# Low halves of every second weight unit on GpSimd instead of VectorE, in the third stage of a streaming encoder layer

## The chip, the cores and the metric

One core of a Trainium2 chip runs the whole program. The metric is device time in microseconds (us) of one execution, the median of several.

## The reference, cut to what matters

One layer over 544 tokens (512 prompt frames and 32 frames of a running stream), width 2048: a combined projection, a convolution branch, an attention branch, a merge, and then a product-key expert layer. The change touches the end of the expert layer:

```python
idx = jnp.take_along_axis(cidx, j, axis=-1)      # 8 heads x 16 experts of 16384 for each token
g = jax.nn.softmax(sc, axis=-1)
ue, ve = u_tab[idx], v_tab[idx]
a = jnp.einsum('td,thkd->thk', xb, ue).astype(f32)
wgt = (g * jax.nn.gelu(a, approximate=False)).astype(xb.dtype)
return jnp.einsum('thk,thkd->td', wgt, ve)
```

All arithmetic is held to float32 accuracy, so the kernel splits each operand of a product in a high half, which TensorE takes exactly, and a low half, the rest, and adds three products.

## The kernel before, in words

All weights stream from HBM in units of 128 x 2048 floats (1 MB): z, attention out, convolution out, merge out and query units first, then 128 units of `peer_u`, then 128 of `peer_v`. Two slots hold raw units (`w_raw`), two the high halves (`w_hi`), two the low halves (`w_lo`). Of a unit: SyncE loads it (line 360, in `load_w`) when the low half of the unit two before it is there, ScalarE rounds it to the high half (line 645) when TensorE is done with the unit two before, and VectorE or GpSimd subtracts (the low half), then TensorE uses it.

Who makes the low half: GpSimd up to the first 42 units of `peer_u`, in four pieces of 512 columns (`lo`, line 590), VectorE in one piece from there on (`split`, line 1319).

The experts are applied in two ways. For 384 tokens all 16384 experts are computed densely by TensorE. For the other 160 the 128 chosen rows of each token are fetched by GpSimd with indirect DMAs (`fetch`, line 618, 1 MB each, 160 slots for the `peer_u` rows and 160 for the `peer_v` rows, three row buffers), and VectorE multiplies them in: `dot` for `peer_u`, `gather_add` (line 1400) for `peer_v`.

The third stage, dense product with `peer_v`, runs over 16 groups of 8 units (0 to 7). In a unit TensorE makes two tiles of 24 matmuls each (line 1822, PSUM `ST`), each of which VectorE adds to `acc` (lines 1384, 1386), and TensorE doesn't begin a tile before the one of the same bank in the unit before has been added. VectorE's order in a unit n of `group` is written out by hand: addition of the first tile; in units 3 to 6 two preparations of the next group's activations (`prep`, lines 1360, 1363, 1365: gate times activation, high half, low half); addition of the second tile; the gathers that `V_SLOTS` puts there; the split of unit n + 2; in group 14 also two residual additions (line 1392). The number of gathers in a group is 8 in group 0, 12 in 1 to 3, 11 in 4, 6, 8, 10, 12 and 14, 10 in 5, 7, 9, 11 and 13, and 0 in 15: one a unit, and a second one in units 0, 2, 1 and 7, in this order, as far as the number asks for it.

GpSimd has only the fetches in this stage: fetch j waits for the gather of j - 3 (`row_taken`), whose buffer it fills. SyncE loads weights, and after each group's eighth weight load, once the eight preparations are done (`w_prepped`), it issues the next gates and activations, `load_ag` (lines 519 and 521, 1.5 MB each), in the same queue as the weights. In group 14 it also has line 559. After group 14 VectorE copies the gathered sums to `rows` (line 1459) and TensorE turns them (line 1838) before group 15. In group 3 VectorE hands over the sums of 32 tokens (`b_handed`), which TensorE turns before group 4 (line 1830).

Of the kernel before, what the change touches and what calls it, by code (L numbers as in the profile page):

```python
# [49 lines left out]
U_PU = U_PQ + NQ  # L50
U_PV = U_PU + NU
# [4 lines left out]
GRP = 8  # L56
NGRP = NKEY // GRP
# [9 lines left out]
SLOTS = SA + SB  # L67
TAIL_DOTS = (2, 2, 2, 2, 2, 1, 1, 1, 1, 1, 1)
V_SLOTS = (8, 12, 12, 12) + (11, 10) * 5 + (11, 0)
NG = 3  # L70
DOTS = 12
LOOP_SLOTS = 21
U_G0 = 42
# [36 lines left out]
def build(nc, w_all, x_t, consts, late, params, lams, keys_t, past_k, past_v, hist,  # L110
          y_t, k_t, v_n, cst_p, cst_s):
    ctx = ExitStack()
    with ctx:
# [168 lines left out]
        def sem(name):  # L282
            return ctx.enter_context(nc.semaphore(name))
# [3 lines left out]
        hi_ready, lo_ready = sem("hi_ready"), sem("lo_ready")  # L287
# [52 lines left out]
        def slot(j):  # L340

            return j if j < SLOTS else (j - SLOTS + SA) % SLOTS

        def slots_at(g, n):

            c, first = V_SLOTS[g], sum(V_SLOTS[:g])
            per = [1 if c else 0] * GRP
            for x in (0, 2, 1, 7)[:max(c - GRP, 0)]:
                per[x] += 1
            first += sum(per[:n])  # L350
            return list(range(first, first + per[n]))
# [224 lines left out]
        @block.gpsimd  # L576
        def _(pool):
            pool.memset(u[:, 0:HIST], 0.0).then_inc(u_zeroed, 1)

            def lo_whole(w, slot):  # L580
                pool.wait_ge(hi_ready, w + 1)
                pool.tensor_tensor(w_lo[:, slot, :], raw[:, slot, :], w_hi[:, slot, :].bitcast(F32), ALU.subtract)\
                    .then_inc(lo_ready, 1)

            def lo(w, slot, nth):

                pool.wait_ge(hi_ready, w + 1)
                for q in range(4):
                    cols = slice(q * UNITW // 4, (q + 1) * UNITW // 4)
                    ins = pool.tensor_tensor(w_lo[:, slot, cols], raw[:, slot, cols], w_hi[:, slot, cols].bitcast(F32), ALU.subtract)  # L590
                    if q < 3:
                        ins.then_inc(lo_part, 1)
                    else:
                        pool.wait_ge(lo_part, nth)
                        ins.then_inc(lo_ready, 1)

            for k in range(1, KD, 2):
                pool.wait_ge(x_loaded[k // 4], 16)
                pool.tensor_tensor(xsq[:, k, :], xs[:, k, :], xs[:, k, :], ALU.mult).then_inc(xsq_pool, 1)
                if k == KD // 2 - 1:  # L600
                    lo_whole(0, 0)
            lo_whole(1, 1)
            with pool.Fori(1, U_PU // 2 + 1) as v:
                for n in range(2):
                    lo(v * 2 + n, n, v * 6 + (3 * n - 3))

            with pool.Fori(0, U_G0 // 2 - 1) as v:
                for n in range(2):
                    lo(v * 2 + (n + U_PU + 2), n, v * 6 + 3 * (n + U_PU + 1))
            nth = 3 * (U_PU + U_G0 - 1)  # L610
            lo(U_PU + U_G0, 0, nth)

            def fetch(j):

                if j >= NG:
                    pool.wait_ge(row_taken, j - NG + 1)
                table = u_rows.rearrange("c b i q n -> (c b i) (q n)") if j < SLOTS else v_rows.rearrange("g c p d -> (g c p) d")
                pool.indirect_dma_start(rows[j % NG][:, :], None, table,  # L618
                                        bass.IndirectOffsetOnAxis(v_idx[:, slot(j):slot(j) + 1], 0))\
                    .then_inc(row_loaded[j % NG], 16)  # L620

            pool.wait_ge(idx_ready, 1 + BG)
            for s in u_stored:
                pool.wait_ge(s, 64 * NKEY // 2 + 1)
            pool.wait_ge(scores_taken, TT)
            pool.wait_ge(chosen, TT)
            for j in range(SLOTS):
                fetch(j)
            pool.wait_ge(rows_stored, 16 * NV)
            for j in range(SLOTS, 2 * SLOTS):  # L630
                fetch(j)


        @block.scalar
# [255 lines left out]
        def _(dve):  # L890
# [154 lines left out]
            with dve.Fori(0, NH // 2) as hp:  # L1045
                own.loop(hp, 2 * per_head)
                turns = iter(range(32))
                for r in range(2):
                    h = hp * 2 + r
                    g = h * STEPS  # L1050
# [265 lines left out]
            def split(un, slot):  # L1316
                dve.wait_ge(hi_ready, un + 1)
                dve.wait_ge(lo_ready, un)
                V.tensor_tensor(w_lo[:, slot, :], raw[:, slot, :], w_hi[:, slot, :].bitcast(F32), ALU.subtract)\  # L1319
                    .then_inc(lo_ready, 1)  # L1320
# [37 lines left out]
            def prep(parity, c):  # L1358
                a = a_st[:, c, :]
                own.by(V.tensor_tensor(a.rearrange("p (b n) -> p b n", n=GB), a.rearrange("p (b n) -> p b n", n=GB),  # L1360
                                       gl_st[:, :, c, :], ALU.mult))
                settle()
                own.by(V.tensor_copy(wt_hi[parity][:, c, :], a))  # L1363
                settle()
                V.tensor_tensor(wt_lo[parity][:, c, :], a, wt_hi[parity][:, c, :].bitcast(F32), ALU.subtract).then_inc(w_prepped, 1)
# [15 lines left out]
            def add(q, d, k, first):  # L1381
                dve.wait_ge(tile_done, q + (2 * KD + 1))
                if first:
                    V.tensor_copy(acc[:, d, 0:NT], PD[k]).then_inc(acc_added, 1)
                else:
                    V.tensor_tensor(acc[:, d, 0:NT], PD[k], acc[:, d, 0:NT], ALU.add).then_inc(acc_added, 1)  # L1386

            def residual(d):

                dve.wait_ge(xr_loaded[d % 2], 16 * (d // 2 + 1))  # L1390
                dve.wait_ge(acc_added, (NGRP - 2) * KD + (d + 3))
                V.tensor_tensor(acc[:, d, 0:NT], gb[:, d % 2, :], acc[:, d, 0:NT], ALU.add).then_inc(xr_taken, 1)

            def gather_add(x, v):

                j = SLOTS + x
                dve.wait_ge(row_loaded[j % NG], v * (16 * LOOP_SLOTS // NG) + 16 * (j // NG + 1))
                dve.wait_ge(row_taken, v * LOOP_SLOTS + j)
                col = slot(j) if x < SB else v * LOOP_SLOTS + slot(j)
                V.scalar_tensor_tensor(acc_g, rows[j % NG][:, :], w_g[:, bass.ds(col, 1)], acc_g, ALU.mult, ALU.add)\  # L1400
                    .then_inc(row_taken, 1)
# [18 lines left out]
            def group(g, g0, v, more, splits, pre=None, first=False, last=False):  # L1420

                parity = g0 % 2
                for n in range(GRP):
                    for k in range(2):
                        q = g * KD + (2 * n + k)
                        dve.wait_ge(acc_added, q + 1)
                        add(q, 2 * n + k, k, first)
                        if k == 0 and more and 3 <= n < 7:
                            if n == 3:
                                dve.wait_ge(al_loaded, g * 16 + 16)  # L1430
                                dve.wait_ge(gl_loaded, g * 16 + 16)
                            prep(1 - parity, 2 * (n - 3))
                            prep(1 - parity, 2 * (n - 3) + 1)
                    if pre and n in pre:
                        pre[n]()
                    for s in slots_at(g0, n):
                        gather_add(s, v)
                    if n < splits:
                        split(g * GRP + (n + U_PV + 2), n % 2)
                    if last:  # L1440
                        residual(2 * n)
                        residual(2 * n + 1)
# [6 lines left out]
            for g in range(4):  # L1449
                group(g, g, 0, True, GRP, {0: b_handed} if g == 3 else None, first=(g == 0))  # L1450
            with dve.Fori(0, (NGRP - 6) // 2) as v:
                own.loop(v, 4 * GRP)
                for b in range(2):
                    group(v * 2 + (b + 4), b + 4, v, True, GRP)
# [6 lines left out]
            def take_back():  # L1461
# [5 lines left out]
                    .then_inc(acc_g_added, 1)  # L1467

            group(NGRP - 2, NGRP - 2, 0, True, GRP, None, last=True)
            hand_over()  # L1470
            dve.wait_ge(xr_taken, KD)
# [462 lines left out]
```

## Time and profile before

| what | us |
| --- | --- |
| median of 3 runs | 4139.95 (4130.86 to 4145.09) |
| the profiled execution, its own time | 4146.39 |
| its span, first to last instruction | 4144.5 |
| TensorE matmuls busy | 3902.2 (94%) |
| VectorE busy | 3103.3 (75%) |
| GpSimd busy | 1372.6 (33%) |
| ScalarE busy | 1057.3 (26%) |
| VectorE's splits, line 1319, 213 of them | 487.3 |
| GpSimd's pieces, line 590, 612 of them | 841.1 |
| third stage, line 1822 | from 2950.6 to 4141 |

The profile is of one execution; the table's busy times are of its span. A busy share is an average over stages with different limits. TensorE's matmuls overlap each other, so that a matmul's own duration (about 0.33 us in this stage) is nearly twice the distance from one to the next. GpSimd's busy time counts its pieces and the writing of its DMA descriptors. Idle time of an engine that nothing waits for costs nothing.

### The profile page before, as it was taken

The page shows a single profiled execution, that of the slowest core. Times are in us where ns is not written, and L with a number is a line of the kernel's source. Part 1 is how long each engine was busy: PE and PEld are TensorE (multiplying, and loading weights), DVE is VectorE, ACT ScalarE, POOL GpSimd, SP SyncE. Part 2 cuts the span into 40 slices and gives each one's busy share as a digit, 9 for nine tenths or more (in the row PEclk, how much of TensorE's full clock was granted, in tenths as well). Part 3 has the DMA queues.
Part 4 walks back from the last instruction along what each step waited for, and adds up shares of the span by engine and source line. Part 5 has one row for each costly group of instructions (what it writes and reads, how often), then busy time and mean ns, then how long its engine had stood idle before and what let it go on. Part 6 is the DMA issues. An engine that isn't in the chain of part 4 may idle for free.

```text
span 4144.5 us, 68649 instructions
## 1 busy us (share of the span) xinstructions
PE 3902.2 (94%) x25123; PEld 3823.2 (92%) x25123; DVE 3103.3 (75%) x4273; ACT 1057.3 (26%) x1096; POOL 1372.6 (33%) x947
## 2 busy tenths in 40 slices
PE   7999999999999998999999999999998989999988
PEld 7889888898899998989999999999998989999988
DVE  6877877788776413477869999996788878888785
ACT  3222222232223112222233333332212222222211
POOL 3333333333334443465642222222133323323220
PEclk9999999999999998999999999999999999999999
DMA  7998989979978986876769999999688887887884
GB/s 284 315 341 307 325 291 351 335 274 345 344 247 290 345 311 227 281 263 229 249 242 387 386 377 392 381 389 385 244 333 309 310 314 292 325 312 296 322 302 150
DMA packets 451447, 1285.21 MB, mean 310 GB/s; under 512 B 34128, under 2 KB 258128, under 8 KB 343120
## 3 DMA queue, kind: packets, MB, share of 16 engines
q1 hardware_dynamic: 372336, 876.99, 59.6%
q0 software_dynamic: 46080, 335.56, 20.9%
q10 hardware_dynamic: 32832, 70.07, 4.4%
q8 instruction: 117, 1.92, 0.2%
q14 instruction: 82, 0.67, 0.0%
HBM read 1070.18 MB, written 345.75 MB: 342 GB/s over the span
## 4 chain that ended last, share of the span: by engine, by line
PE 45%; DVE 17%; issue 16%; DMA 11%; POOL 5%; SPq 3%; ACT 1%; DVEq 1%; POOLq 0%; ACTq 0%
PE ST L1732 17%; PE PA L1489 16%; PE ST L1822 9%; DMA w_raw<-w_all 6%; POOL w_lo L590 5%; DVE w_lo L1319 4%; DMA u_rows<-u_out 4%; DVE xg L1023 3%; DVE PA L1400 2%; PE ST L1797 2%; SPq L389 1%; DVE a_st L1360 1%; DVE u_out L926 1%; DVE acc L1386 1%; DVE wt_hi L1363 1%
## 5 line engine op out<-in xcount | busy, mean ns | idle before, releaser
L590 POOL TENSOR_TENSOR w_lo<-w_raw,w_hi 128x512 fp32r<-128x512 f32 x612 | 841.1, 1406 | 1243.4 <-ACT w_hi L645 1243.4
L645 ACT ACTIVATE w_hi<-w_raw 128x2048 fp32r<-128x2048 f32 x368 | 703.4, 1912 | 1451.7 <-PE ST L1822 634.5
L1822 PE MATMUL ST<-wt_hi,w_hi 128*128 128x384 f32 x2048 | 698.9, 341 | 77.2 <-DVE acc L1386 74.4
L1822 PE MATMUL ST<-wt_lo,w_hi 128*128 128x384 f32 x2048 | 695.4, 340 | 0.0
L1822 PE MATMUL ST<-wt_hi,w_lo 128*128 128x384 f32 x2048 | 694.6, 339 | 0.0
L1319 DVE TENSOR_TENSOR w_lo<-w_raw,w_hi 128x2048 fp32r<-128x2048 f32 x213 | 487.3, 2288 | 189.0 <-ACT w_hi L645 189.0
L618 POOL DMA_INDIRECT rows<-v_rows,v_idx x160 | 331.8, 2074 | 813.4 <-DVE PA L1400 783.2
L1489 PE MATMUL PA<-h_hi,w_hi 128*128 128x272 f32 x2496 | 546.3, 301 | 6.4 <-POOL w_lo L590 6.4
L1489 PE MATMUL PA<-h_hi,w_lo 128*128 128x272 f32 x2496 | 527.0, 293 | 0.0
L1489 PE MATMUL PA<-h_lo,w_hi 128*128 128x272 f32 x2496 | 526.4, 293 | 0.0
L1732 PE MATMUL ST<-h_hi,w_hi 128*128 128x384 f32 x1408 | 509.6, 362 | 5.9 <-DVE w_lo L1319 4.3
L1732 PE MATMUL ST<-h_hi,w_lo 128*128 128x384 f32 x1408 | 476.4, 338 | 0.0
L1732 PE MATMUL ST<-h_lo,w_hi 128*128 128x384 f32 x1408 | 474.6, 337 | 0.0
L1822 PEld LDWEIGHTS ST<-wt_hi,w_hi 128*128 128x128 f32 x2048 | 393.2, 192 | 85.1 <-DVE acc L1386 42.0
L1489 PEld LDWEIGHTS PA<-h_hi,w_hi 128*128 128x128 f32 x2496 | 405.5, 194 | 13.2 <-issue 6.7
L926 DVE STREAM_TRANSPOSE u_out<-u_in 128x2048 f32<-128x2048 f32 x128 | 294.9, 2306 | 162.0 <-DMA u_rows<-u_out 153.0
L1489 PEld LDWEIGHTS PA<-h_lo,w_hi 128*128 128x128 f32 x2496 | 404.1, 194 | 0.0
L1489 PEld LDWEIGHTS PA<-h_hi,w_lo 128*128 128x128 f32 x2496 | 401.2, 194 | 0.0
L1822 PEld LDWEIGHTS ST<-wt_lo,w_hi 128*128 128x128 f32 x2048 | 393.0, 192 | 0.0
L1822 PEld LDWEIGHTS ST<-wt_hi,w_lo 128*128 128x128 f32 x2048 | 392.9, 192 | 0.0
L1400 DVE SCALAR_TENSOR_TENSOR PA<-rows,w_g,PA 128x2048 f32<-128x2048 f32 x160 | 375.8, 2349 | 5.3 <-DVE PA L1400 0.8
L618 POOL DMA_INDIRECT rows<-u_rows,v_idx x160 | 178.2, 1114 | 600.7 <-DVE rows L1327 593.6
(271 smaller groups left out, 6293.2 us busy)
## 6 DMA issues: line engine op xcount, KB each, us to landing
w_raw<-w_all SPq DMA_DIRECT2D x368, 1024.0 KB
u_in<-w_all SPq DMA_DIRECT2D x128, 1024.0 KB, 8.5
u_rows<-u_out SPq DMA_DIRECT2D x512, 256.0 KB, 7.4
v_rows<-w_all SPq DMA_DIRECT2D x128, 1024.0 KB, 9.1
a_scr<-gb ACTq DMA_DIRECT2D x128, 192.0 KB
g_scr<-g_st ACTq DMA_DIRECT2D x24, 1024.0 KB, 12.0
a_st<-a_scr SPq DMA_DIRECT2D x15, 1536.0 KB, 8.4
gl_st<-g_scr SPq DMA_DIRECT2D x15, 1536.0 KB
```

Source lines behind the costliest of these rows:

```text
L389: sp.dma_start(u_rows[bass.ds(hp * 32 + i, 1), :, :, q, :].rearrange("a b i n -> i (a b) n"), u_out[32 * q:32 * q + 32, i % 2, :].rearrang ...
L590: ins = pool.tensor_tensor(w_lo[:, slot, cols], raw[:, slot, cols], w_hi[:, slot, cols].bitcast(F32), ALU.subtract)
L618: pool.indirect_dma_start(rows[j % NG][:, :], None, table, bass.IndirectOffsetOnAxis(v_idx[:, slot(j):slot(j) + 1], 0))\
L645: act.activation(w_hi[:, slot, :], raw[:, slot, :], ACT.Copy).then_inc(hi_ready, 1)
L926: V.transpose(u_out[:, i % 2, :].rearrange("p (b k j) -> p k b j", b=4, k=KD), u_in[:, i % 2, :])\
L1023: own.by(V.scalar_tensor_tensor(xg[:, a:b], src, cw, xg[:, a:b], ALU.mult, ALU.add))
L1319: V.tensor_tensor(w_lo[:, slot, :], raw[:, slot, :], w_hi[:, slot, :].bitcast(F32), ALU.subtract)\
L1400: V.scalar_tensor_tensor(acc_g, rows[j % NG][:, :], w_g[:, bass.ds(col, 1)], acc_g, ALU.mult, ALU.add)\
L1489: last = mm(out[:, f, :], a, rhs, start=(x == 0 and y == 0), stop=(x == n - 1 and y == 2))
L1732: last = mm(dst[n], a, b[:, k, 0:NT], start=(k == 0 and y == 0), stop=(k == KD - 1 and y == 2))
L1797: last = mm(out, oh2[:, sl, :], oh1[:, sl, :], start=True, stop=True)
L1822: last = mm(PD[k], a, r_[b][:, c, :], start=(c == 0 and y == 0), stop=(c == GRP - 1 and y == 2))
```

## The change

In the third stage VectorE splits only units with even n; for odd n GpSimd makes the low half with its `lo`, four pieces, each time before the fetches of that unit. The fetches stay in their order: the first three (`NG`) ahead of all, then each one after the gather that frees its buffer. In group 15 there are six low halves to make, so three of them on GpSimd.

```diff
@@ -627,8 +627,20 @@
             for j in range(SLOTS):
                 fetch(j)
             pool.wait_ge(rows_stored, 16 * NV)
-            for j in range(SLOTS, 2 * SLOTS):
+            for j in range(SLOTS, SLOTS + NG):
                 fetch(j)
+
+            def v_pool(g, los):
+                for n in range(GRP):
+                    if n % 2 and n < los:
+                        pool.wait_ge(lo_ready, g * GRP + (n + U_PV + 2))
+                        lo(g * GRP + (n + U_PV + 2), n % 2, g * (3 * GRP // 2) + 3 * (U_PU + U_G0 + n // 2))
+                    for s in slots_at(g, n):
+                        if SLOTS + s + NG < 2 * SLOTS:
+                            fetch(SLOTS + s + NG)
+
+            for g in range(NGRP):
+                v_pool(g, GRP if g < NGRP - 1 else GRP - 2)
@@ -1435,7 +1447,7 @@
                         pre[n]()
                     for s in slots_at(g0, n):
                         gather_add(s, v)
-                    if n < splits:
+                    if n < splits and n % 2 == 0:
                         split(g * GRP + (n + U_PV + 2), n % 2)
                     if last:
                         residual(2 * n)
```

## Rows read from the trace of the kernel before

**Rows 1.** Waits of TensorE, whole span: us in total, times, longest us

```profile
PE ST L1822 <- DVE acc L1386: 74.4, 18, 14.7
```

**Rows 2.** The chain that ended last, third stage: start us, us, what

```profile
3038.03 12.73 PE ST L1822 x72
...
3392.16 16.64 DMA w_raw<-w_all
...
3413.67 11.37 PE ST L1822 x48
...
3922.22 11.36 PE ST L1822 x48
...
4006.54 10.26 PE ST L1822 x48
...
4074.55 66.86 PE ST L1822 x384
```

**Rows 3.** Stretches around one stop: us, then each engine's busy us, PEclk, DMA share, GB/s

```profile
3409.40:3413.60 4.20, 0.08 (x1) 0.00 (x0) 2.75 (x3) 1.33 (x1) 0.00 (x0) 0.91 1.03 429
3413.70:3420.70 7.00, 7.00 (x24) 7.00 (x25) 6.86 (x4) 1.91 (x1) 2.52 (x2) 0.57 0.92 331
```

**Rows 4.** VectorE's timeline, groups 5 and 6: start us, us, instruction, idle before

```profile
3386.45 0.56 DVE L1365 TENSOR_TENSOR wt_lo<-a_st,wt_hi 128x384 fp32r<-128x384 f32 x1
...
3425.53 4.85 DVE L1400 SCALAR_TENSOR_TENSOR PA<-rows,w_g,PA 128x2048 f32<-128x2048 f32 x2
3430.29 2.29 DVE L1319 TENSOR_TENSOR w_lo<-w_raw,w_hi 128x2048 fp32r<-128x2048 f32 x1
...
3438.60 2.28 DVE L1319 TENSOR_TENSOR w_lo<-w_raw,w_hi 128x2048 fp32r<-128x2048 f32 x1
```

**Rows 5.** SyncE's timeline, the burst between groups 5 and 6

```profile
3387.19 0.38 SPq L519 DMA_DIRECT2D a_st<-a_scr  x1
...
3392.16 8.40 SPq L360 DMA_DIRECT2D w_raw<-w_all  x2
```

**Rows 6.** DMA queues, first 3387.2 to 3404.2, then 3429.7 to 3433.2: packets, MB, share

```profile
q1 hardware_dynamic: 4177, 3.54, 66.7%
q0 software_dynamic: 362, 2.70, 39.8%
...
q0 software_dynamic: 144, 1.05, 87.4%
```

**Rows 7.** VectorE's timeline, merge stage: the same subtraction alone and beside GpSimd's pieces

```profile
1313.06 0.73 DVE L1154 TENSOR_TENSOR m_lo<-ly,m_hi 128x544 f32 x1
...
1317.92 1.61 DVE L1154 TENSOR_TENSOR m_lo<-ly,m_hi 128x544 f32 x1
```

**Rows 8.** ScalarE's timeline, third stage

```profile
3392.87 1.92 ACT L645 ACTIVATE w_hi<-w_raw 128x2048 fp32r<-128x2048 f32 x1 [6.30 <-PE ST L1822]
```

**Rows 9.** GpSimd's timeline, four pieces each, in the merge and `peer_u` stages

```profile
1314.48 6.20 POOL L590 TENSOR_TENSOR w_lo<-w_raw,w_hi 128x512 fp32r<-128x512 f32 x4 [4.83 <-ACT w_hi L645]
...
1939.97 5.02 POOL L590 TENSOR_TENSOR w_lo<-w_raw,w_hi 128x512 fp32r<-128x512 f32 x4 [6.00 <-ACT w_hi L645]
...
1968.87 7.06 POOL L590 TENSOR_TENSOR w_lo<-w_raw,w_hi 128x512 fp32r<-128x512 f32 x4 [3.28 <-ACT w_hi L645]
```

**Rows 10.** GpSimd's timeline, fetches of the third stage

```profile
3395.97 2.75 POOL L618 DMA_INDIRECT rows<-v_rows,v_idx  x1 [3.22 <-DVE PA L1400]
...
3416.61 0.94 POOL L618 DMA_INDIRECT rows<-v_rows,v_idx  x1 [8.88 <-DVE PA L1400]
...
3428.15 0.94 POOL L618 DMA_INDIRECT rows<-v_rows,v_idx  x1 [6.31 <-DVE PA L1400]
```

**Rows 11.** VectorE's timeline, group 14

```profile
4031.33 2.29 DVE L1319 TENSOR_TENSOR w_lo<-w_raw,w_hi 128x2048 fp32r<-128x2048 f32 x1
...
4040.57 2.29 DVE L1319 TENSOR_TENSOR w_lo<-w_raw,w_hi 128x2048 fp32r<-128x2048 f32 x1
...
4065.39 2.29 DVE L1319 TENSOR_TENSOR w_lo<-w_raw,w_hi 128x2048 fp32r<-128x2048 f32 x1
```

## The prediction, made blind

> **What bounds the kernel now.** Third stage only; nothing before it is touched. I read the waits of TensorE, the chain, the stretches around one stall, then each engine's timeline there. TensorE's largest wait in this stage is on VectorE's addition of a finished tile: 74.4 us in only 18 waits [rows 1]. So it is not a steady drag but a few long stops. The chain shows where [rows 2]: when nothing stops it, TensorE does eight units (384 matmuls, the last group) in 66.86 us, 8.36 us a unit. From unit 2 of group 1 (3038.03) to unit 2 of group 13 (3922.22) there are 12 groups in 884.2 us, 73.7 each, so 6.8 lost per group; from group 6 on (3413.67 to 3922.22, 7 groups) 72.65 each, 5.8 lost; and 84.3 for the next one (to 4006.54). Every loss is at the same place, before unit 2 of a group: in group 6 the load of that unit's weights took 16.64 us, then ScalarE's high half 1.92 us, VectorE's low half, and TensorE restarted at 3413.67. In the stretch before the restart TensorE did one matmul in 4.2 us, and after it 24 matmuls took 7.00 us, at a granted clock of 0.57 [rows 3]; at full pace 24 take 4.18. So a stop of 4.3 us costs another 2.8 here, nearer 1.6 in most groups (5.8 less the stop of about 4.1).
>
> Why is that load late? SyncE issues the load of the next gates and activations (3 MB) once VectorE has prepared the last of a group's weights, ending at 3387.0 [rows 4]; issue at 3387.19, and the unit-2 weights behind it in the same queue at 3392.16 [rows 5]. From 3387.2 to 3404.2 that queue moved 3.54 MB and the row gathers 2.70 MB, at full engines, and only then the weights came [rows 6]. **The bound per group is this burst**; elsewhere TensorE is full, and VectorE just keeps pace with it: in units 3 to 6 its splits come 8.31 us apart (3430.29, 3438.60), with additions, two preparations and a gather between them and no idle time [rows 4].
>
> **The change, part by part.**
> Removed from VectorE: 63 splits of 2.29 us [rows 4], those of the odd units. VectorE is on the path only in two ways.
> (1) *It reaches the last preparation sooner, so the burst starts sooner.* In units 3 to 6 two splits go, 4.6 us. But GpSimd's pieces run beside the preparations of units 4 and 6. Nearest rows, from the merge stage: a VectorE subtraction that takes 0.73 us alone took 1.61 us beside GpSimd's pieces, 0.88 more [rows 7]. About three such operations collide, 2.6 us. Bounds: 0 (they miss each other) and 6 operations, 5.3 us. I take 2.6, so the burst starts 1.5 to 2 us sooner.
> (2) *The gathers move out of it.* GpSimd's low half starts when ScalarE's high half ends. That one starts when TensorE ends a unit and takes 1.92 us [rows 8]; with 0.2 for signals, an allowance of mine, the pieces start 2.1 us after the unit. Four pieces take 5.02 us undisturbed [rows 9], to 7.2 us. The fetch that followed unit 7's gather at 3395.97 [rows 10] would then issue at about 3399.9, 4 us later. Its 1 MB, which takes 3.4 us of the engines alone [rows 6], mostly leaves the stretch that the burst needs. Together I expect the unit-2 weights 4.5 us sooner (bounds: 1.5, the start alone, and 6). The stop is 4.3, so in groups 6 to 13 it goes, with its slow matmuls: 8 x 5.8 = 46 us. Groups 2, 3 and 5 have stops longer than 4.5, so 4.5 each, 13.5; group 14's, 17.4 in all, also 4.5. I give nothing to group 4, whose restart follows the hand-over of 32 rows' sums. **Sum: -64 us.**
>
> Added to GpSimd: 63 times four pieces, in front of the fetches of the same unit on its queue.
> (3) *TensorE's need of an odd unit.* 2.1 + 5.02 = 7.2 us after a unit ends, against 8.36 when it is wanted: 1.2 to spare. Beside VectorE's preparations four pieces took 6.20 us in the merge stage [rows 9], so 8.3: just due. I charge 0.3 us for each of the two units a group that collide (bounds 0 and 1.0): 30 x 0.3, **+9 us**. What a row shows is a partial wait on either side. The Trainium skill, page "SBUF — State Buffer", section "SBUF: two separate sides", says that the pair of ports is an exclusive lock and the loser blocks for the whole instruction; by that a collision costs VectorE up to a whole piece, 1.26 us, not 0.88, and by an estimate from it this term would be some 20 and the total near -31. The rows show lock-like growth of both, but less than a whole piece.
> (4) *Fetches queued behind the pieces.* In nine groups (1 to 4 and the even ones) unit 1 has two gathers, and the fetch behind the first brings the row that unit 2's second gather uses. Before: issued at 3416.61 [rows 10], used after 3428.0 (the second of a pair starting at 3425.53) [rows 4], 11.4 us. After: it waits until the low half is done, 3.5 us later, and TensorE's stop no longer gives it time. From the unit-1 end: issue at 7.2, use at 8.36 + 2.9 = 11.3, 4 us. A fetch takes 0.94 us to write and its packets ended 5 us after issue when alone (issued at 3428.15 [rows 10], all 144 moved by 3433.2 [rows 6]), or more beside a weight load. So VectorE waits 1 to 3.5 us, then gathers, splits unit 4 and is 1 to 3 us late for TensorE, which had 0.6 to spare. 9 x 2, **+18 us** (bounds 0 and 9 x 5). All other fetches slip 2 to 4 us against rows used 10 us and more after landing: nothing.
> (5) *Group 14.* There VectorE also adds the residual and sets a pace of 9.24 us a unit (4031.33 to 4040.57) [rows 11], 0.9 over TensorE's. Without every second split it is below it: four units, -3.5. And the split at 4065.39 stands right before the copy for which TensorE waits: -2.3. **-5.8 us.** In group 15 odd units come 5.02 against 2.29 us after the high half, with 8.36 to have it in: nothing.
> SyncE's weight loads of odd slots now wait for GpSimd's last piece, 7.2 us after a unit. After unit 7 that is 3399.9, where VectorE had done by 3397.9; but that load was held by the burst's issue anyway (two weight loads from 3392.16 to 3400.56 [rows 5]): nothing. More instructions on GpSimd's queue: nothing, it is idle for most of the stage; were they to count they would be in (3).
>
> Sum: -64 + 9 + 18 - 5.8 = -43 us. The profiled execution took 4146.4 us (span 4144.5); the median of the runs shown is 4139.95. So 4103 for such an execution, **4097 us** against the median.
>
> **The rivals.**
> *The burst does not move.* If the engines' total traffic, not order, sets when the unit-2 weights land, stops stay, and only (3), (4) and (5) are left; with stops in place (4) has its slack back and costs at most half: +9 + 9 - 6 = +12, near 4145 (4135 to 4152). For it: the engines are full from 3387 to 3409 [rows 6]. Against: before 3387 they are not, and the gathers have a later deadline.
> *GpSimd late at every odd unit: slower.* Place: the low half of units 1, 3, 5, 7. Price: four pieces took 7.06 us beside VectorE's selection [rows 9]; 2.1 + 7.06 = 9.2, 0.8 late, 63 times, 53 us, and (4) grows by 2 a group to 36. With -64 and -6 that is +19, 4159. It decides from about 6.25 us for four pieces on average. For it: the spare time is 1.2 us, and the preparations are just such operations. Against: they overlap the pieces in only half of the odd units, and gathers, which read PSUM, seem not to hold anything: fetches beside them take 0.94 us, beside splits 2.75 [rows 10]. The Trainium skill, "GPSIMD Engine Reference", section "4.1 Engine selection", advises VectorE for elementwise work because GpSimd is about twice as slow; on the lengths the trace agrees (5.02 against 2.29), and it would make the time worse only in this rival, since both fit under a unit otherwise.
> *More than forecast.* No late rows and no collisions: -64 - 6 = -70, 4070.
> That the change does not do what it says has no hold: 63 splits leave one queue for another.
>
> **How the numbers follow.** Forecast 0.55 (its own range 4080 to 4118: (1) and (2) together between -45 and -80, (4) between 0 and 30); more 0.15; burst unmoved 0.16; GpSimd late 0.14. A measurement of this kernel tells about 0.3%, 12 us. Faster by more: 0.55 + 0.15 + a little of the unmoved case = 0.72. Within: 0.13 of the unmoved case = 0.13. Slower: GpSimd late and the rest = 0.15. The range leaves out the best end of "more" and most of "GpSimd late": 4062 to 4150.
>
> **What would show it.** Right: eight groups of the chain near 67 to 69 us, granted clock 1.0 after unit 2's start; the 3 MB load issued 1.5 to 2 us nearer the end of unit 5; a VectorE wait for rows in unit 2 of even groups; group 14's splits no longer 9.24 apart. Wrong: TensorE waiting for GpSimd's low half at odd units in most groups, four pieces at 6.3 us or more, or restarts before unit 2 with loads still over 16 us.

## The result, and the profile after

The changed kernel takes **4149.79 us** (median of 11 runs, 4143.75 to 4158.71) against 4141.8 for the kernel before (11 runs, 4130.86 to 4148.77): a ratio of 1.0025, 95% interval 1.0014 to 1.0036. Forecast was 4097. The gain did not come, and a small loss did. The profiled execution of the changed kernel has a span of 4147.9 us. In the two profiles the third stage, from its first matmul (2950.6 before, 2939.5 after) to the end of the span, takes 1193.9 us before and 1208.4 after; the stages ahead of it, which the change leaves alone, differ by 11 us the other way. So the profiles are compared stretch by stretch below, and the whole is told by the medians.

The work moved as the change says. These are three groups of the page of the changed kernel (busy us, mean ns of one, then idle time before them):

```profile
L590 POOL TENSOR_TENSOR w_lo<-w_raw,w_hi 128x512 fp32r<-128x512 f32 x864 | 1168.7, 1385 | 1509.9 <-ACT w_hi L657 1509.8
...
L1331 DVE TENSOR_TENSOR w_lo<-w_raw,w_hi 128x2048 fp32r<-128x2048 f32 x150 | 343.2, 2288 | 152.3 <-ACT w_hi L657 152.3
...
L618 POOL DMA_INDIRECT rows<-v_rows,v_idx x160 | 234.0, 1463 | 411.2 <-DVE PA L1412 375.1
```

63 splits left VectorE (213 to 150) and 252 pieces came to GpSimd (612 to 864). In the code, lines from 632 on are 12 higher than before: the matmuls are L1834, the additions L1396 and L1398, the gathers L1412. What TensorE and VectorE wait for in the third stage (us in total, times, longest):

```profile
PE ST L1834 <- DVE acc L1398: 86.6, 28, 14.8
...
PE PA L1850 <- DVE rows L1471: 7.6, 1, 7.6
```

```profile
DVE PA L1412 <- DMA rows<-v_rows,v_idx: 29.1, 9, 7.4
```

TensorE's wait was 74.4 us in 18 pieces [rows 1]; now it is longer, and in 28. VectorE's wait for fetched rows is new: the trace before has none in this stage.

**Where in the stage.** The stretches from the first matmul of group 6 to the first of group 14 tell it best: eight groups, four with 11 gathers and four with 10. The columns are us, then busy us and count of PE, PEld, DVE, ACT and POOL, then granted clock, DMA share and GB/s. Before:

```profile
3392.70:3975.10 582.40, 551.19 (x3074) 547.84 (x3073) 484.28 (x468) 122.80 (x64) 179.42 (x85) 0.97 0.83 310
```

After:

```profile
3389.00:3979.50 590.50, 550.70 (x3074) 545.31 (x3073) 456.52 (x436) 122.84 (x64) 289.21 (x212) 0.97 0.81 305
```

At 8.36 us a unit, 64 units take 535.0 us. Before, 47.4 us were lost here (the prediction said 46); after, 55.5. VectorE is 28 us less busy and the time is 8 us longer. Groups 1 to 5 went from 373.0 to 378.8 in the same view, and group 14 from 99.1 to 97.5.

**What got better: the stop before unit 2.** ScalarE's timeline at group 8; the first row is the high half of unit 1, which starts 0.2 us after TensorE ends unit 7, the second that of unit 2, which starts as its weights land. Before:

```profile
3539.55 1.92 ACT L645 ACTIVATE w_hi<-w_raw 128x2048 fp32r<-128x2048 f32 x1 [6.31 <-PE ST L1822]
3554.98 1.91 ACT L645 ACTIVATE w_hi<-w_raw 128x2048 fp32r<-128x2048 f32 x1 [13.51 <-DMA w_raw<-w_all]
```

After:

```profile
3535.95 1.92 ACT L657 ACTIVATE w_hi<-w_raw 128x2048 fp32r<-128x2048 f32 x1 [6.31 <-PE ST L1834]
3549.57 1.92 ACT L657 ACTIVATE w_hi<-w_raw 128x2048 fp32r<-128x2048 f32 x1 [11.71 <-DMA w_raw<-w_all]
```

The distance went from 15.43 to 13.62 us: the weights land 1.8 us sooner (the mean over groups 6 to 13 went from 15.66 to 13.91). TensorE is out of work 16.5 us after the first of these rows, and from the landing it takes 1.92 (high half), 0.1, 2.29 (split) and 0.5 (VectorE's addition, which stands behind the split) until it may go on, 4.8 in all. So the weights are due at 11.7: 3.7 late before, 1.9 late after. The restart after, from TensorE's timeline with the idle time in brackets, says the same, and its first matmuls are back at 0.33 us at once:

```profile
3554.43 0.45 PE L1834 MATMUL ST<-wt_hi,w_hi 128*128 128x384 f32 x1 [1.88 <-DVE acc L1398]
...
3554.89 0.33 PE L1834 MATMUL ST<-wt_hi,w_lo 128*128 128x384 f32 x1
```

**What got worse: a new stop before unit 4, two units later, in the groups with a second gather in unit 1.** GpSimd's timeline of group 8 (the bracket is idle time and what ended it; x4 is the four pieces of one unit):

```profile
3556.67 5.02 POOL L590 TENSOR_TENSOR w_lo<-w_raw,w_hi 128x512 fp32r<-128x512 f32 x4 [5.88 <-ACT w_hi L657]
3561.85 0.95 POOL L618 DMA_INDIRECT rows<-v_rows,v_idx  x1 [0.15 <-issue]
...
3572.03 2.73 POOL L618 DMA_INDIRECT rows<-v_rows,v_idx  x1 [4.95 <-DVE PA L1412]
3574.79 4.96 POOL L590 TENSOR_TENSOR w_lo<-w_raw,w_hi 128x512 fp32r<-128x512 f32 x4
```

VectorE's timeline at the same place:

```profile
3563.53 2.35 DVE L1412 SCALAR_TENSOR_TENSOR PA<-rows,w_g,PA 128x2048 f32<-128x2048 f32 x1
3569.41 2.36 DVE L1412 SCALAR_TENSOR_TENSOR PA<-rows,w_g,PA 128x2048 f32<-128x2048 f32 x1 [3.53 <-DMA rows<-v_rows,v_idx]
3571.67 2.28 DVE L1331 TENSOR_TENSOR w_lo<-w_raw,w_hi 128x2048 fp32r<-128x2048 f32 x1
3573.87 0.55 DVE L1398 TENSOR_TENSOR acc<-ST,acc 128x384 f32<-128x384 f32 x1
3574.34 5.83 DVE L1372 TENSOR_TENSOR a_st<-a_st,gl_st 128x384 f32<-128x384 f32 x1
```

And TensorE's two restarts that follow:

```profile
3574.48 0.69 PE L1834 MATMUL ST<-wt_hi,w_hi 128*128 128x384 f32 x1 [3.13 <-DVE acc L1398]
3574.96 0.52 PE L1834 MATMUL ST<-wt_lo,w_hi 128*128 128x384 f32 x1
...
3583.14 0.44 PE L1834 MATMUL ST<-wt_hi,w_hi 128*128 128x384 f32 x1 [1.40 <-DVE acc L1398]
```

Read them in order. The fetch at 3561.85 has stood behind unit 1's four pieces. Its row is wanted at 3565.9 and lands 3.53 us later. The gather, the split and the addition for which TensorE waits all move by that much, so TensorE stops for 3.13 us and does its next matmuls at 0.52 us, as it did after the stops of before [rows 3]. By then the pieces that GpSimd makes during unit 3 are due too, and VectorE's first preparation, whose median is 0.55 us, takes 5.83: until the last of the four is done. That makes the second stop, 1.40. In group 10 the two are 3.31 and 4.23. The 5.83 us kind is in groups 8, 10 and 12. In group 6 the row is late by 1.85 us and the first stop is 1.46; there the pieces lengthen four preparation operations by about 1 us each instead (0.36 to 0.56 us alone), and the second stop is 2.90. One of the four, and TensorE's restart after the second stop:

```profile
3431.22 1.64 DVE L1372 TENSOR_TENSOR a_st<-a_st,gl_st 128x384 f32<-128x384 f32 x1
```

```profile
3436.26 0.44 PE L1834 MATMUL ST<-wt_hi,w_hi 128*128 128x384 f32 x1 [2.90 <-DVE acc L1398]
```

So each of the four groups with a late row has two new stops.

### The profile page after: what moved, and what is told of

Read it like the earlier page. It is cut to its first block, busy times and chain, and to the rows that moved or that the text cites. A ratio compares the mean times of both kernels' runs of the same rounds, so it can differ in the third digit from the quotient of the medians.

```text
span 4147.9 us, 68857 instructions
## 1 busy us (share of the span) xinstructions
PE 3902.0 (94%) x25123; PEld 3819.6 (92%) x25123; DVE 3032.8 (73%) x4210; ACT 1057.9 (26%) x1096; POOL 1606.1 (39%) x1199
## 3 DMA queue, kind: packets, MB, share of 16 engines
q8 instruction: 117, 1.92, 0.2%
## 4 chain that ended last, share of the span: by engine, by line
PE 51%; issue 15%; DVE 12%; DMA 11%; POOL 7%; SPq 3%; ACT 1%; DVEq 1%; POOLq 0%; ACTq 0%
PE PA L1501 16%; PE ST L1744 16%; PE ST L1834 14%; POOL w_lo L590 7%; DMA u_rows<-u_out 4%; DVE xg L1035 3%; DMA rows<-v_rows,v_idx 3%; DMA w_raw<-w_all 3%; PE ST L1809 2%; SPq L389 1%; DVE u_out L938 1%; ACT w_hi L657 1%; DVE a_st L1372 1%; DVE w_lo L1331 1%; DMA rows<-u_rows,v_idx 1%
## 5 line engine op out<-in xcount | busy, mean ns | idle before, releaser
L590 POOL TENSOR_TENSOR w_lo<-w_raw,w_hi 128x512 fp32r<-128x512 f32 x864 | 1168.7, 1385 | 1509.9 <-ACT w_hi L657 1509.8
L1834 PE MATMUL ST<-wt_hi,w_hi 128*128 128x384 f32 x2048 | 700.4, 342 | 89.5 <-DVE acc L1398 86.6
L1834 PE MATMUL ST<-wt_hi,w_lo 128*128 128x384 f32 x2048 | 695.7, 340 | 0.0
L1834 PE MATMUL ST<-wt_lo,w_hi 128*128 128x384 f32 x2048 | 695.3, 340 | 0.0
L1834 PEld LDWEIGHTS ST<-wt_hi,w_hi 128*128 128x128 f32 x2048 | 394.0, 192 | 100.0 <-DVE acc L1398 57.9
L1331 DVE TENSOR_TENSOR w_lo<-w_raw,w_hi 128x2048 fp32r<-128x2048 f32 x150 | 343.2, 2288 | 152.3 <-ACT w_hi L657 152.3
L1412 DVE SCALAR_TENSOR_TENSOR PA<-rows,w_g,PA 128x2048 f32<-128x2048 f32 x160 | 375.7, 2348 | 33.1 <-DMA rows<-v_rows,v_idx 29.1
L1834 PEld LDWEIGHTS ST<-wt_lo,w_hi 128*128 128x128 f32 x2048 | 393.9, 192 | 0.0
L618 POOL DMA_INDIRECT rows<-v_rows,v_idx x160 | 234.0, 1463 | 411.2 <-DVE PA L1412 375.1
L1834 PEld LDWEIGHTS ST<-wt_hi,w_lo 128*128 128x128 f32 x2048 | 392.8, 192 | 0.0
## 6 DMA issues: line engine op xcount, KB each, us to landing
g_scr<-g_st ACTq DMA_DIRECT2D x24, 1024.0 KB, 11.7
```

Of the source, the lines that this page charges most:

```text
L618: pool.indirect_dma_start(rows[j % NG][:, :], None, table, bass.IndirectOffsetOnAxis(v_idx[:, slot(j):slot(j) + 1], 0))\
L1834: last = mm(PD[k], a, r_[b][:, c, :], start=(c == 0 and y == 0), stop=(c == GRP - 1 and y == 2))
```

## The experiments

All ratios are to the kernel before, with 95% intervals, and no kernel leaves any work out. "Groups 6 to 13" is the stretch shown above; its full-pace length is 535.0 us.

### Unit 1 back on VectorE

In this text a set of units says during which units GpSimd makes a low half (that of the unit two later). The variants have the changed kernel's function in this form, each with its own set, and VectorE splits the rest. The count that `lo` waits for is kept in step, in lines not shown.

```diff
-                    if n % 2 and n < los:
+                    if n in (3, 5, 7) and n < los:
...
-                    if n < splits and n % 2 == 0:
+                    if n < splits and n not in (3, 5, 7):
```

> GpSimd makes the low halves in units 3, 5 and 7 only; VectorE keeps unit 1. Theory R (the changed kernel loses where the fetch behind unit 1's pieces brings a row too late for unit 2; that wait makes VectorE late and its next preparation then stands behind four pieces): no VectorE wait for rows over 1 us, no preparation over 2 us, 35 to 40 us less than the changed kernel, so about 4110 to 4118. Rival C (the pieces of units 3 and 5 block the preparations by themselves, whatever the rows do): preparations of 5 us and more stay in the even groups and the time stays within 10 us of the changed kernel's 4150.

Measured: 4113.63 us, ratio **0.9937** (0.9923 to 0.9951).

```profile
3395.90:3953.50 557.60, 539.76 (x3075) 536.63 (x3074) 458.14 (x444) 122.89 (x64) 265.57 (x180) 0.99 0.86 323
```

One unit in four moved back turns the loss into a gain of 0.9% against the changed kernel, 32.9 us of it in groups 6 to 13. VectorE waits for no row there, and its longest preparation multiply (ns min/median/max) falls from 5864 to 1566, though GpSimd still makes its pieces during units 3, 5 and 7, those of 3 and 5 beside the preparations. The changed kernel's line, then this one's:

```profile
L1372 DVE TENSOR_TENSOR a_st<-a_st,gl_st x128: 541/551/5864, 2918.3 to 4058.7; 128x384 f32<-128x384 f32 x128
```

```profile
L1378 DVE TENSOR_TENSOR a_st<-a_st,gl_st x128: 545/551/1566, 2933.8 to 4033.8; 128x384 f32<-128x384 f32 x128
```

So the loss hangs on unit 1's pieces, and not on pieces beside the preparations as such.

### Unit 1 alone, unit 7 alone, units 3 and 5 alone

The sets are (1,), (7,) and (3, 5).

> GpSimd makes the low half in unit 1 only. Theory R: the fetch still stands behind the pieces, but nothing starts the burst sooner, so the stop before unit 2 stays at about 4.3 us and gives the late row most of its time: row waits of 0 to 2 us, no long preparation because no pieces run in unit 3, 4140 to 4155. Rival C: as the kernel before, 4138 to 4144, with no row waits.

> GpSimd makes the low half in unit 7 only, so that alone the fetch of unit 7 moves out of the burst by 4 us. If it is bytes that set when the unit-2 weights land (as the prediction had it), they land 2 to 3 us sooner against the end of unit 7 and the time falls by 20 to 30 us, to about 4115. If the burst is bound by its own small pieces (512 bytes each), the landing moves by less than 1 us and the time by less than 10.

> GpSimd makes the low halves in units 3 and 5 only: the burst starts sooner, no fetch leaves it. If the sooner start is what shortened the stops in the changed kernel, the 3 MB load is issued about 1.1 us sooner against the end of unit 7 and the stops in groups 6 to 13 fall from 4.1 to about 3, the time by 10 to 20 us. Rival C: preparations of 5 us in the even groups, time at or above the kernel before.

Measured: unit 1 alone 4147.42 us, **1.0020** (1.0011 to 1.0029); unit 7 alone 4106.95, **0.9924** (0.9908 to 0.9941); units 3 and 5 alone 4144.47, **1.0011** (0.9997 to 1.0024). The same stretch of each, unit 1 alone:

```profile
3387.50:3974.90 587.40, 552.64 (x3075) 548.33 (x3074) 467.07 (x460) 122.79 (x64) 205.10 (x117) 0.97 0.81 307
```

Unit 7 alone:

```profile
3375.50:3932.10 556.60, 539.92 (x3073) 536.64 (x3072) 467.07 (x460) 122.91 (x64) 205.34 (x117) 0.99 0.86 324
```

Units 3 and 5 alone:

```profile
3385.00:3965.40 580.40, 549.78 (x3073) 546.63 (x3072) 475.25 (x452) 122.82 (x64) 239.38 (x148) 0.97 0.83 311
```

Against 582.4 before, unit 7 gives 25.8 us, units 3 and 5 give 2.0, and unit 1 costs 5.0. The parts do not add up: with unit 7's gain already in, unit 1 costs 33 (590.5 against 557.6). The reason is slack. With unit 1 alone TensorE still stops 3.6 to 3.9 us before unit 2; the rows are up to 1.9 us late there and each costs a stop of 0.9 to 1.5. With the first stop down to about 2 us, as in the changed kernel, the same fetch is up to 3.7 us late and costs two stops.

What unit 7 does is seen in GpSimd's timeline: the fetch behind unit 7's gather, before and with unit 7 alone (group 7 to 8).

```profile
3542.64 2.74 POOL L618 DMA_INDIRECT rows<-v_rows,v_idx  x1 [3.20 <-DVE PA L1400]
```

```profile
3517.70 5.03 POOL L590 TENSOR_TENSOR w_lo<-w_raw,w_hi 128x512 fp32r<-128x512 f32 x4 [2.17 <-ACT w_hi L663]
3522.87 0.95 POOL L618 DMA_INDIRECT rows<-v_rows,v_idx  x1
```

Measured from unit 1's high half (3539.55 before; 3515.63 here) the fetch moved from 3.09 to 7.24 us, and unit 2's high half from 15.43 to 14.17 (means over groups 6 to 13: 15.66 and 13.84).

The sooner start of the burst is what units 3 and 5 give alone: 3 MB issued 6.6 us before the end of unit 7 instead of 5.5. Alone it is worth nothing that shows: unit 2's high half starts 15.50 us after unit 1's there (mean over groups 6 to 13 15.59, against 15.66 before). The second half of those 3 MB took about as much longer to land. With units 3 and 5 on GpSimd (line 521, us from issue to landing, min, median, max):

```profile
DMA to landing us min/median/max: 12.5/16.9/23.3
```

With unit 7 alone:

```profile
DMA to landing us min/median/max: 12.4/15.8/17.2
```

### The fetch ahead of the pieces

In unit 1 of the changed kernel the first fetch goes before GpSimd's pieces instead of behind them; then in unit 5, with units 3 and 5 alone on GpSimd. The first edit, against the kernel with units 3, 5 and 7 (in the second it is `n == 5` and the set (3, 5)):

```diff
-                    ahead = 0 if n in (3, 5, 7) else 0
+                    ahead = 1 if n == 1 else 0
                     todo = [SLOTS + s + NG for s in slots_at(g, n) if SLOTS + s + NG < 2 * SLOTS]
                     for j in todo[:ahead]:
                         fetch(j)
-                    if n in (3, 5, 7) and n < los:
+                    if n in (1, 3, 5, 7) and n < los:
...
-                    if n < splits and n not in (3, 5, 7):
+                    if n < splits and n not in (1, 3, 5, 7):
```

> As the changed kernel, with one thing swapped: in unit 1 GpSimd issues the fetch behind the first gather before the four pieces, not after them. Theory R: the row is there in time, so no row wait over 1 us in unit 2 of the even groups from 6 on, no preparation over 2 us; the pieces come about 1 us later, which the unit after the stop has time for. 4110 to 4120. Rival (the split's length itself, four pieces of 5 us in unit 1, makes TensorE late): 4145 or more.

> As the run with pieces in units 3 and 5, but in unit 5 the fetch goes before the pieces again. Theory B (bytes in front of the unit-2 weights decide; there the sooner start of the burst was given back by the fetch of unit 5, which slid into it): high half of unit 2 starts about 1 us sooner against the end of unit 7 than 15.8, stops 3 instead of 4, 4125 to 4135. Rival (the start of the burst does not matter at all): 15.8 as before, 4138 to 4146.

Measured: unit 1's fetch first 4120.7 us, **0.9953** (0.9939 to 0.9967); units 3 and 5 with unit 5's fetch first 4114.2, **0.9933** (0.9918 to 0.9948). TensorE's waits in groups 6 to 13, of the first:

```profile
PE ST L1840 <- DVE acc L1404: 17.4, 8, 3.1
PE ST L1840 <- POOL w_lo L590: 1.7, 4, 0.4
```

Of the second:

```profile
PE ST L1840 <- POOL w_lo L590: 19.7, 8, 2.5
PE ST L1840 <- DVE acc L1404: 3.9, 4, 1.8
```

The first keeps the changed kernel's division of work and is 29 us faster than it: the order of one fetch and four pieces was the fault. What is left to it is small, GpSimd 0.4 us late for unit 3. The second came out below its forecast of 4125 to 4135, and does not tell what it was made for. Behind the fetch the low half for unit 7 came late, so TensorE stopped 2.5 us before unit 7 in every group, and the burst found more room before unit 2. The stop was moved and grew smaller. It says nothing clean on the sooner start.

### The wait alone: no work moved

All splits stay on VectorE, and `ahead` is 0. The only thing that changes is that the fetches behind unit 7's gathers wait until TensorE has ended unit 0 of the next group:

```diff
+                    if n == GRP - 1 and todo:
+                        pool.wait_ge(tile_done, 2 * KD + (g + 1) * KD + 2)
                     for j in todo[ahead:]:
                         fetch(j)
```

> VectorE makes every low half, as in the kernel before; the only edit is that GpSimd's fetch of unit 7 waits until TensorE has ended unit 0 of the next group, 5 us later than it was. Theory B: all of the gain of the run with pieces in unit 7 comes from the fetch's place, so the stop before unit 2 falls to 2 us or less and the time to 4100 to 4112, unless the row is then late for unit 1, which VectorE has 3 us to spare for. Rival (the gain came from VectorE's freed 2.3 us in unit 7): 4138 to 4146.

Measured: 4102.87 us, ratio **0.9905** (0.9891 to 0.9920).

```profile
3384.60:3930.30 545.70, 535.37 (x3075) 532.01 (x3073) 484.24 (x468) 122.92 (x64) 165.31 (x85) 1.00 0.88 331
```

36.7 us of the 47.4 lost in groups 6 to 13 are back, with VectorE as busy as before (484 us) and a granted clock of 1.00. GpSimd's fetch now waits for TensorE:

```profile
3529.57 0.94 POOL L618 DMA_INDIRECT rows<-v_rows,v_idx  x1 [8.66 <-PE ST L1842]
```

That is 8.55 us after unit 1's high half (3521.02), and unit 2's starts at 13.39. What the low half moved in unit 7 did was to be such a delay.

The later fetch has a price of its own in the first groups. Groups 1 to 3 have two gathers in unit 7, and in groups 2 to 4 VectorE now waits for a row 8.0, 3.6 and 3.3 us. Group 2, ScalarE's high half of unit 2, then VectorE up to the low half:

```profile
3095.10 1.92 ACT L665 ACTIVATE w_hi<-w_raw 128x2048 fp32r<-128x2048 f32 x1 [12.73 <-DMA w_raw<-w_all]
```

```profile
3099.68 2.36 DVE L1420 SCALAR_TENSOR_TENSOR PA<-rows,w_g,PA 128x2048 f32<-128x2048 f32 x1 [8.02 <-DMA rows<-v_rows,v_idx]
3101.94 2.28 DVE L1339 TENSOR_TENSOR w_lo<-w_raw,w_hi 128x2048 fp32r<-128x2048 f32 x1
```

The weights are there, and the split stands behind the late gather. TensorE's stops in groups 2 and 3 are 7.7 and 7.9 us against 9.3 and 7.2 before, and groups 1 to 5 take 371.2 us against 373.0. Unit 7 alone, whose fetch is less late, has the same waits (7.3, 3.0 and 0.9) and 366.0 us.

### The load order

All splits on VectorE, fetches as before; SyncE issues unit 2's weights ahead of the 3 MB instead of behind them.

```diff
             with sp.Fori(1, NGRP - 2) as g:
-                for n in range(GRP):
+                for n in range(1, GRP + 1):
                     sp.wait_ge(lo_ready, g * GRP + (n + 1 + U_PV))
                     load_w(g * (GRP // 2) + (U_PV // 2 + 1 + n // 2), n % 2)
                 sp.wait_ge(w_prepped, g * GRP + 2 * GRP)
                 load_ag(g + 2)
...
```

> VectorE makes every low half; SyncE issues the unit-2 weights before the 3 MB of gates and activations instead of behind them. If the burst in front of these weights is the whole of the stop before unit 2, that stop goes in groups 2 to 13 (5.8 to 8 us each with its slow matmuls) and the unit-3 weights, now the first behind the burst, are late by 0 to 3 us: 4075 to 4105. If the load only waits elsewhere, the stop moves to unit 3 in full: 4130 to 4145.

Measured: 4140.81 us, ratio **0.9995** (0.9984 to 1.0006). ScalarE's timeline, units 1, 2 and 3 of group 8:

```profile
3544.25 1.92 ACT L664 ACTIVATE w_hi<-w_raw 128x2048 fp32r<-128x2048 f32 x1 [6.31 <-PE ST L1841]
3552.66 1.92 ACT L664 ACTIVATE w_hi<-w_raw 128x2048 fp32r<-128x2048 f32 x1 [6.49 <-PE ST L1841]
3565.87 1.92 ACT L664 ACTIVATE w_hi<-w_raw 128x2048 fp32r<-128x2048 f32 x1 [11.29 <-DMA w_raw<-w_all]
```

Unit 2's weights are in time (8.41 us, TensorE's own pace), and unit 3's are late instead (13.21 here, 12.40 to 19.15 over groups 6 to 13). The first forecast, 4075 to 4105, took unit 3 to be late by 3 us at most; the second, that the stop moves to unit 3 in full, was met. But more than the order changed. Unit 2's load waits for the low half of unit 0, and the 3 MB now stand behind it:

```profile
3541.72 0.38 SPq L519 DMA_DIRECT2D a_st<-a_scr  x1
```

They start 2.3 us before the end of unit 7 here, and 0.4 to 2.3 over groups 6 to 13, not 5.5, and VectorE waits for rows four times in groups 6 to 13, 9.9 us in total. So the run shows that this order moves the stop and brings nothing; what the order would do with an equally early start is not shown. Taking unit 7's fetch, whose deadline is later, out of the stretch did help.

### Both, and a second burst

Units 3, 5 and 7 on GpSimd with the wait of the run before; and, on VectorE alone with that wait, the load of line 559 moved from the head of group 14 to behind its fifth weight load:

```diff
-            sp.dma_start(xg_res[:, :, :], x2_scr[:, :, NT:T].rearrange("c p n -> p c n")).then_inc(xg_loaded, 16)
             for n in range(2 * GRP - 2):
                 sp.wait_ge(lo_ready, (NGRP - 2) * GRP + n + 1 + U_PV)
                 load_w((NGRP - 2) * (GRP // 2) + U_PV // 2 + 1 + n // 2, n % 2)
+                if n == 4:
+                    sp.dma_start(xg_res[:, :, :], x2_scr[:, :, NT:T].rearrange("c p n -> p c n")).then_inc(xg_loaded, 16)
```

> GpSimd makes the low halves of units 3, 5 and 7, and the fetch behind unit 7 waits, as in the run with the wait alone, until TensorE ends unit 0 of the next group. It asks whether the moved work is worth anything once the fetch stands where it should. Theory W (the place of unit 7's fetch is the whole gain, VectorE's lighter load is worth nothing because TensorE is not waiting for it): within 5 us of the run with the wait alone, ratio 0.989 to 0.992, stops before unit 2 of 1.2 to 2 us. Theory V (VectorE's lighter load adds its own gain through the 1.1 us sooner load and group 14's pace): 0.988 or less. Theory C (pieces beside preparations hold VectorE or GpSimd and cost TensorE something): 0.9925 or more, with stops at odd units or at units 4 and 6.

> All splits on VectorE, unit 7's fetch waits as before, and SyncE's load on line 559 (the residual of the turned sums, whose issue held SyncE 8.8 to 11 us right behind the last burst) is issued in the middle of group 14, behind its fifth weight load. Theory Q (group 14's stop of 15 us before unit 2 comes from this load standing in the same queue ahead of the unit-2 weights): the stop falls to the 1.5 us of the other groups and the time by 10 to 15 us, ratio 0.987 to 0.988. Rival: the load holds the weights wherever it stands, since its issue alone takes 9 us: a stop of 8 us or more moves to unit 7 of group 14 or unit 0 of group 15 and the ratio stays at 0.990 to 0.992.

Measured: both together 4106.41 us, **0.9908** (0.9891 to 0.9924), and 546.6 us in groups 6 to 13 against 545.7 with the wait alone; unit 2's high half starts 13.20 us after unit 1's in the mean, against 13.05. Moving three low halves in four off VectorE adds nothing that these runs can see, though the 3 MB start 1.1 us sooner.

The later load: 4090.3 us, **0.9881** (0.9861 to 0.9900), the fastest kernel of this study. Its median is 12.6 us below that of the wait alone, which ran on another chip; the intervals of the two ratios overlap, so the traces decide. SyncE's timeline, the load with the wait alone, then in this one:

```profile
3926.03 8.80 SPq L559 DMA_DIRECT2D xg_res<-x_scr  x1
```

```profile
3964.79 0.72 SPq L563 DMA_DIRECT2D xg_res<-x_scr  x1
```

Group 14, with the wait alone:

```profile
3930.30:4029.90 99.60, 73.14 (x402) 71.36 (x401) 76.29 (x79) 17.25 (x9) 15.73 (x10) 0.88 0.78 280
```

With the load moved too:

```profile
3922.30:4012.70 90.40, 73.45 (x402) 71.67 (x401) 76.44 (x79) 17.25 (x9) 15.97 (x10) 0.91 0.85 308
```

9.2 us come out of group 14. TensorE's stop before unit 2 is 5.5 us there instead of 15.0; it did not fall to the 1.5 of the other groups, as the forecast had it. No new stop is seen. The longest wait of the stage is now the one of group 2, 7.8 us.

## Why the prediction was wrong, point by point

**What bounds the kernel: right.** The loss per group is the burst before unit 2, and groups 6 to 13 lost 47.4 us by the stretch, forecast 46.

**What failed, in the terms of the sum.** -64 + 9 + 18 - 5.8 was forecast. Two terms were mis-sized, both past their own bounds: (1) and (2) together, forecast -64 (bounds -45 and -80), are worth about -34 by the run with unit 7 alone; and (4), forecast +18 (bounds 0 and 30 in the range), is +36 in the medians, 32.9 of it in groups 6 to 13. The first miss is some 30 us and the second 18. By the sum neither alone makes a loss: with (4) at 18 the time would have been near 4132, with (1) and (2) at -64 near 4120.

**Step (1), the burst starts sooner: the size was off and no gain came of it.** Forecast 1.5 to 2 us sooner, measured 1.1 (6.6 us before unit 7's end instead of 5.5 [rows 5, 8]). Its value was never priced alone. The collisions taken off it were as forecast, two or three operations a group, 0.9 to 1.1 us longer each. Units 3 and 5 alone, and the run with the wait and three units moved, both show that a start 1.1 us sooner does not bring unit 2's weights sooner: the second half of the 3 MB took 16.8 us to land instead of 15.7 (the two kernels with the wait).

**Step (2), the gathers move out: right in kind, the step that failed most in size.** The fetch moved by 4.15 us, forecast 4. But the weights came 1.8 us sooner, not 4.5, near the lower bound of 1.5. I took 4.5 by letting the whole 1 MB leave the stretch and adding the start; a fetch issued 7.4 us after the end of unit 7 still has its packets beside the weights, which land at 13.8. Groups 6 to 13 gave 25.8 us with unit 7 alone and 36.7 with the fetch later still, where the forecast had 46. Groups 2 and 3 were to give 4.5 each: with unit 7 alone their stops went from 9.3 and 7.2 us to 7.1 and 7.4.

**Step (3), collisions: forecast 9 us, measured between nothing and 7.** With unit 1 left out, three units on GpSimd cost 1.0 us over eight groups against one (557.6 and 556.6); the medians differ by 7, with ratios whose intervals overlap (0.9937 and 0.9924). Four pieces took 5.0 to 5.8 us in the stage of the changed kernel and TensorE waited for no low half of GpSimd there. The price shows once VectorE is late: in the 5.83 us preparations and in group 6's four lengthened ones.

**Step (4), fetches behind the pieces: place, cause and wait right, price wrong; this is what makes a loss of the gain that was left.** It is unit 2's second gather in the groups with two gathers in unit 1, waiting 1 to 3.5 us by forecast and 1.9 to 3.7 in the four such groups of 6 to 13 (12.7 us together). I put 2 us on each of nine groups, 18; unit 1 costs 32.9 us in those four, 8.2 each, and 36 in the medians (4149.8 against 4113.6). TensorE's waits give the parts: the first stop, 1.5 to 3.3 us, was in the forecast (11.1 us in four); the second, 1.4 to 4.2 (11.4 in four), was not, since I did not see that a late VectorE comes upon the pieces of unit 3; and the 10 us that remain are slow matmuls, such as those at 0.52 us behind the long stops (TensorE's busy time is 10.9 us more for the same matmuls, 550.70 against 539.76), which I had charged for the stops of before and forgot here. That all other late fetches cost nothing failed too: in groups 2 to 4 VectorE waits for rows in every kernel that moves unit 7's fetch.

**Step (5), group 14: forecast 5.8 from the pace of [rows 11], measured 1.6** (99.1 to 97.5 us), 1.0 of it at the hand-over (TensorE's wait for the copy, 8.6 to 7.6 us). The group's large stop came for the greater part from the load on line 559, which the prediction did not name: moved, it took the stop from 15.0 to 5.5.

**Together**, in medians: unit 7 alone brings 34 us (4106.95 against 4140.97), units 3 and 5 on top of it take up to 7 back, and unit 1 takes 36. The rival with the nearest time is the unmoved burst; its +12 stands on record as "near 4145" and is 4152 on the median of 4139.95. Its nearness is luck: it held that a late row costs less while the stops stay, which unit 1 alone bears out, and that the stops stay, which they did not. The rival of a late GpSimd fell: the bound of 6.25 us for four pieces was never met. The rival of 4070 had rows in time and the whole -64; with the row in time the kernel took 4120.7.

**Still open:** why a sooner issue of the 3 MB does not end sooner, and why the preparation was held for four pieces and not one, were not tried by themselves.

## What to carry to other kernels

When work is put in front of a DMA issue on an engine's queue, price the transfer behind it by its own deadline, and with the slack that will be left once the change has worked, not with today's. Before moving work off an engine to shift a transfer, shift the transfer alone: one wait gave 0.95% here, and the moved work on top of it nothing. If the transfers ahead of a deadline are too many, look for one that is wanted later and delay it, and check its own deadline in every kind of group: here the same wait held VectorE 8 us in group 2. Changing the order of the loads moved the stop and gained nothing.

## What the runs showed of the hardware

**One VectorE operation held over four GpSimd instructions.** The stretch of that preparation in the changed kernel, same columns as above:

```profile
3574.70:3580.20 5.50, 5.50 (x18) 5.50 (x19) 5.48 (x1) 0.00 (x0) 5.03 (x5) 0.50 0.89 341
```

TensorE's granted clock is 0.50, the lower of its two levels (1.2 GHz), after the 3.13 us stop. VectorE has a single instruction in it, begun at 3574.34, 0.45 us before the first piece at 3574.79, and ended 0.4 us after the last. GpSimd was writing a fetch's descriptors until 3574.76, so the pieces followed without a gap; it was the same in groups 10 and 12. In group 6 the multiply also began beside the end of such a write (3428.79), but the pieces came 0.34 us after the write, and it took 0.55. In the three runs with pieces beside the preparations in which VectorE was not late, the same multiply took at most 1.6 us. The Trainium skill, "SBUF — State Buffer", "SBUF: two separate sides", says that whichever starts first has the shared ports for its whole instruction and the other blocks; by that the multiply would have lost nothing, or at most one piece, 1.26 us, had it come second. Here it lost 5.3 us over four in a row, so the measurement decides. That back-to-back pieces keep the ports from one to the next would explain it, and is not shown.

**The time to write a fetch's descriptors depends on VectorE.** 0.95 us alone, 2.73 beside a split, as in [rows 10]; in the changed kernel, where fewer splits lie beside them, the `peer_v` fetches took 234.0 us together, against 331.8 before.

**The issue of one DMA can hold SyncE for long.** The load on line 559 took 8.80 us to issue right behind 3 MB with the wait alone (11.06 in the kernel before, 13.75 in the changed one), and 0.72 us in the middle of the group. In each of these timelines SyncE's next load starts only when it is issued.
